# The key-side forget bias of one attention group: from a broadcast tensor added on VectorE to an extra matmul into the score bank

## The reference

```python
def dense_causal_attention(q, k, v, scale, fcum=None):
    ...
        s = jnp.einsum('bhqd,bhkd->bhqk', qi, k, preferred_element_type=jnp.float32) * scale
        if fcum is not None:
            s = s + args[2][..., :, None] - fcum[:, :, None, :]
        qpos = i * Q_BLOCK + jnp.arange(Q_BLOCK)
        s = jnp.where(kpos[None, :] <= qpos[:, None], s, NEG_INF)
        p = jax.nn.softmax(s, axis=-1)
        return jnp.einsum('bhqk,bhkd->bhqd', p.astype(v.dtype), v)

def fox_mixer(q, k, v, f_logit, b_f):
    log_f = jax.nn.log_sigmoid(f_logit.astype(jnp.float32) + b_f.astype(jnp.float32))
    fcum = jnp.cumsum(log_f, axis=1).transpose(0, 2, 1)
```

## Time and profile before

| | |
|---|---|
| median of three runs | 3331.21 us |
| the profiled execution, its own time | 3331.21 us |
| its span, first to last instruction | 3329.4 us |
| TensorE matmul busy | 3042.9 us, 91% |
| VectorE busy | 1924.9 us, 58% |
| ScalarE busy | 1279.9 us, 38% |
| GpSimd busy | 372.0 us, 11% |
| mean granted TensorE clock | 0.987 of full speed |
| fox heads, from the first score to the last | about 178 to 222 us |

### The profile page before, as it was taken

How to read it: one execution, slowest core, us unless ns; L and a number is a source line. 1 busy time by engine, 2 the same in 40 slices (tenths; PEclk the granted TensorE clock), 3 DMA queues, 4 the chain that set the end, 5 groups by cost and what they waited for, 6 DMA issues and landing times.

```text
span 3329.4 us, 43391 instructions
## 1 busy us (share of the span) xinstructions
PE 3042.9 (91%) x18036; PEld 2379.4 (71%) x18036; DVE 1924.9 (58%) x2872; ACT 1279.9 (38%) x2355; POOL 372.0 (11%) x364
## 2 busy tenths in 40 slices
PE   8999999999999999999999999999987777777776
PEld 8888978999999999989999997444442233333332
DVE  6565665555555555676765454555555555555654
ACT  4554554444434345565544352222222222222222
POOL 1001000000000001100000011222232222222221
PEclk9999999999999999999999999999999989999999
DMA  7454446555555555544445448999999999999997
GB/s 216 174 195 158 161 151 215 179 188 179 188 179 186 181 182 198 195 165 153 152 177 203 140 152 333 430 431 430 431 430 431 430 429 431 431 431 431 431 431 337
DMA packets 94785, 912.65 MB, mean 274 GB/s; under 512 B 10416, under 2 KB 14904, under 8 KB 19580
## 3 DMA queue, kind: packets, MB, share of 16 engines
q0 software_dynamic: 38128, 541.61, 38.1%
q1 hardware_dynamic: 48816, 344.95, 29.9%
q10 hardware_dynamic: 7644, 23.30, 2.2%
HBM read 900.38 MB, written 9.45 MB: 273 GB/s over the span
## 4 chain that ended last, share of the span: by engine, by line
PE 66%; DMA 23%; DVE 6%; ACT 4%; issue 1%; ACTq 0%; POOL 0%; DVEq 0%; POOLq 0%
PE sums L555 15%; PE sums L557 14%; PE sums L556 14%; DMA area<-in_uv,cst 13%; PE sums L1025 9%; DMA hT<-in_uv,cst 5%; DMA ringx<-in_uv,cst 3%; PE sums L981 2%; DVE area L2261 1%; PE sums L617 1%; DVE wl L1690 1%; PE sums L619 1%; PE sums L618 1%; ACT cst L1070 1%; ACT area L1070 1%
## 5 line engine op out<-in xcount | busy, mean ns | idle before, releaser
L1690 DVE TENSOR_TENSOR wl<-ring,wh 128x1024 fp32r<-128x1024 f32 x612 | 749.9, 1230 | 597.2 <-ACT wh L1070 596.3
L1070 ACT ACTIVATE wh<-ring 128x1024 fp32r<-128x1024 f32 x612 | 643.5, 1054 | 460.2 <-PE sums L557 404.5
L1070 ACT ACTIVATE cst<-cst 128x1 f32<-128x1 f32 (+2 forms) x786 | 234.2, 299 | 903.6 <-DVE cst L2261 845.1
L1025 PE MATMUL sums<-area,cst 128*128 128x512 f32 x984 | 457.4, 611 | 100.1 <-ACT cst L1070 99.8
L1025 PEld LDWEIGHTS sums<-area,cst 128*128 128x128 f32 x984 | 182.7, 193 | 356.6 <-issue 189.6
L2261 DVE CUSTOM_DVE_ANT_0 area<-area 128x2048 f32<-128x2048 f32 x123 | 281.8, 2291 | 254.5 <-DMA area<-in_uv,cst 254.5
L555 PE MATMUL sums<-normed,wh 128*128 128x256 f32 x1440 | 407.0, 283 | 0.2 <-DVE wl L1690 0.2
L557 PE MATMUL sums<-normed,wl 128*128 128x256 f32 x1440 | 406.7, 282 | 0.0
L1025 PE MATMUL sums<-ringx,cst 128*128 128x512 f32 x656 | 303.8, 609 | 60.0 <-ACT cst L1070 60.0
L555 PE MATMUL sums<-hidden,wh 128*128 128x256 f32 x1024 | 289.8, 283 | 0.0
L556 PE MATMUL sums<-hidden,wh 128*128 128x256 f32 x1024 | 289.8, 283 | 0.0
(11 more groups left out here) (335 smaller groups left out, 5753.6 us busy)
## 6 DMA issues: line engine op xcount, KB each, us to landing
ring<-in_w_in_a SPq DMA_DIRECT2D x66, 1024.0 KB, 4.9
ring<-in_w_up SPq DMA_DIRECT2D x64, 1024.0 KB, 4.9
ring<-in_w_down SPq DMA_DIRECT2D x64, 1024.0 KB, 4.9
ring<-in_w_out SPq DMA_DIRECT2D x32, 1024.0 KB, 5.0
ring<-in_w_in_b SPq DMA_DIRECT2D x16, 1024.0 KB, 4.9
ring<-in_w_xk SPq DMA_DIRECT2D x16, 1024.0 KB, 5.2
ring<-in_w_xv SPq DMA_DIRECT2D x16, 1024.0 KB, 5.1
ring<-in_w_xq SPq DMA_DIRECT2D x16, 1024.0 KB, 5.0
```

What stands on the lines that cost most here:

```text
L1025: mm = te.matmul(sums[t][:, 512 * i:512 * i + 512], diag[:, n % 2, :], v[:, 512 * i:512 * i + 512], start=False, stop=n % 128 == 127)
L1070: return sc.activation(out, in_, f, **kw)
L1690: ve.tensor_tensor(wl[:, j % 3, :], ring[:, load % 3, j % 2 * 1024:j % 2 * 1024 + 1024], wh[:, j % 3, :], ALU.subtract).then_inc(lo_in, 1)
```

## The change

The broadcast of the key-side term goes. Each score matmul of a fox head is left open for accumulation, and a second matmul adds to the same columns of the same bank: its weights are the head's block of `sel8` (8 partitions, 128 columns), its moving operand `nfcum` (8 partitions, 128 or 256 columns). The product is row h of `nfcum` on all 128 partitions. VectorE's L1813 then adds the query column and the causal mask, which is the constant that MLA heads use. The DMA to HBM and back, their waits, the buffer `fb` and the eight `mask_keys` are removed; the count on `bias_in` becomes 48 where it was 96; GpSimd's wait for `brow_out` moves behind its eight subtractions.

```diff
-        fb = flat(bias)[:, 2048:5120].rearrange("p (h n) -> p h n", h=8)
-        nfcum_d = nc.dram_tensor("fox_rows", (8, T), F32).ap()
...
-                                bias=fb[:, h, :], f=h, out=cqm[:, 4 + h // 2, :]))
+                                bias=causal, f=h, out=cqm[:, 4 + h // 2, :]))
...
                             hd, bank = heads[x + e], banks[3 + e]
+                            f = "f" in hd
                             mm = te.matmul(bank[:, a:b], hd["q"][:, qt * P:(qt + 1) * P], hd["k"][:, 0:b - a],
-                                           start=True, stop=True)
+                                           start=True, stop=not f)
+                            if f:
+                                mm = te.matmul(bank[:, a:b], C("sel8", 128, 128 * hd["f"], 8), nfcum[:, 0:b - a],
+                                               start=False, stop=True)
                             if qt == 1:
                                 mm.then_inc(scored, 1)
...
-                on.wait_ge(bias_in, 96)
+                on.wait_ge(bias_in, 48)
...
                         if "f" in hd:
                             on.wait_ge(fcol, 2)
-                            on.wait_ge(fox_v, hd["f"] + 2)
...
-                        if x + 1 < n and "f" in heads[x + 1]:
-                            mask_keys(x + 1)
...
-            def mask_keys(h):
-
-                ve.tensor_tensor(fb[:, h, :], fb[:, h, :], causal, ALU.add).then_inc(fox_v, 1)
...
-                on.wait_ge(bias_in, 48)
-                mask_keys(0)
                 yield from attention(fox_heads(), 8)
...
             sum_squares("attn")
-            on.wait_ge(brow_out, 16)
-            on.wait_ge(fox_in, 1)
-            gp.dma_start(nfcum_d, nfcum[:, :]).then_inc(bias_in, 16)
-            on.wait_ge(bias_in, 16)
-            for y, n in ((0, 128), (128, 256)):
-                gp.dma_start(fb[:, :, y:y + n], bass.AP(nfcum_d.tensor, 0, [[0, 128], [T, 8], [1, n]])
-                             ).then_inc(bias_in, 16)
             for k in range(1, 16, 2):
                 on.wait_ge(xh_in, SPLIT_H["mem"] + k + 1)
                 gp.tensor_tensor(m1l[:, k, :], memT[:, k, :], m1h[:, k, :], ALU.subtract).then_inc(xl_p, 1)
+            on.wait_ge(brow_out, 16)
             on.wait_ge(moved, 2)
```

## The result

The changed kernel takes 3355.86 us (median of 4 runs, 3352.16 to 3357.42) beside 3331.62 us for the kernel before (4 runs, 3328.55 to 3336.02): ratio 1.0066, 95% interval 1.0055 to 1.0079. That is 24 us slower. The forecast of 3344.5 us had the direction and little over half of the size, and the median lies above the range.

A forecast was written before the change was run, and what follows sets the result against it. TensorE, full in the fox heads, was taken to bound the kernel; removals cost nothing, four pairs add 3.3 us each, 13.3 in all: 3331.2 + 13.3 = 3344.5 us. Own range 3341 to 3348, wider range 3336 to 3350.

The forecast's parts named there:

- The bound: Fox heads, 178 to 222.5 us: TensorE sets the time, busy 44.50 of 44.50 us, never waiting for another engine.
- What is removed: Eight VectorE mask additions, 4.4 us, and the DMA round trip: covered by TensorE's work, so costed at nothing.
- The rival of VectorE's relief: Fox heads: VectorE was near the bound, so the eight masks count 4.4 us, giving 3326.8 us; chance 0.03.
- The 4.18 us of a pair: A pair of fox scores on TensorE: 4 x 0.415 + 4 x 0.63 = 4.18 us, where it was 0.86.
- 0.20 us for each change of shape: TensorE, between 8-row and 64-row matmuls: each border costs 0.09 us of emptying plus 0.11 of bare weight load.
- The cheap rival: Fox pairs: 8 rows beside 64 are no change of shape, TensorE keeps its pipeline full; 3336.4 or 3338.9 us, chance 0.15.
- The lock of VectorE and TensorE: Fox pairs: banks held longer and L1813's wait delay split weights, 1 to 2 us a pair; 3348 to 3353 us, chance 0.06.
- The step that failed: Low clock of 0.50 at 304 to 308 us: that stretch moves as a whole, its length differing by a microsecond or two.
- a predicted 13.3 us: TensorE, four pairs of fox scores: 3.3 us added to each pair, 13.3 us in all.

The follow-up runs named there:

- the one-pair kernel: The changed kernel with the selector matmuls of the first two fox heads alone, the other six heads' key bias left out; 3339.14 us, ratio 1.0017.

## Why the prediction was wrong in size

**The bound** was right. TensorE stayed busy for 63.70 of 63.70 us and no other engine ended a wait of it.

**What is removed** was rightly costed at nothing, by experiment: 1.0005 (0.9996 to 1.0014) without the selectors. The rival of VectorE's relief (3326.8 us) is out. VectorE's busy time in the fox stage fell by 3.5 us (39.00 to 35.46) where 4.4 were forecast; it bought nothing either way.

**The 4.18 us of a pair** were right to 0.02 in the second and third pair, and so was its smallest brick, 0.20 us for each change of shape. It came from two places of one timeline, and four kernels now bear it out: pairs with 9 changes at 4.16, with 5 at 2.75, with 5 and side-by-side selectors at 2.11, and with 5 and doubled selectors at 4.06. The split of the 0.20 into 0.09 of emptying and 0.11 of bare load was not tested by itself. The cheap rival is out too.

**The lock of VectorE and TensorE** did not come: the splits idled 17.0 us instead of 7.7, more slack and not less.

**The step that failed** is the one on the clock: the sum has no term for it in the fox stage, and its only word on a low clock is about the stretch from 304 to 308 us. It read: "That stretch moves as a whole; how long it lasts may differ by a microsecond or two." I had looked for the clock only where it was already low, and summed the new pairs and all that follows them at 2.4 GHz because the window of before stood at 1.00. The clock is the missing term of the sum: 13.4 us at half clock inside the fox stage, 6.0 us of time, beside a predicted 13.3 us. The kernel with 128-row selectors is the forecast made real: all the changes of shape but one, no fall of the clock, 12.6 us on the stage.

The Trainium skill, TensorE: Matmul & The Clock Gate, Part 1: The HAM clock gate, describes a clock that idleness of TensorE brings down. The trace of before fits that, 0.50 after a window busy for 2.00 of 4 us; the changed kernel's busy row does not, since TensorE is busy for 4.00 of 4.00 us from 178 to 182 and from 222 to 226 us, ahead of the first and the last fall. But that row counts each matmul until its results are written and so hides the holes. By the prices of the passes, 8 x 0.107 + 8 x 0.215, an estimate, only 2.57 of a pair's 4.16 us are streaming. The holes don't order the kernels either: the selectors of 128 rows stream in 2.57 of 3.87 us and had no fall, the doubled ones, by the same estimate, in 0.64 + 2.57 = 3.21 of 4.06 us, and the clock fell at all four pairs. A reader who looks for idle time alone would make my mistake.

**Behind the stage** the difference shrinks from 18.8 us (fifteenth split) to 16.4 (121st). A part of it is the low stretch near 300 us that both kernels have. Windows of the kernel before:

```profile
302.60:312.80 10.20, 10.20 (x142) 9.90 (x139) 0.00 (x0) 0.64 (x3) 0.00 (x0) 0.50 0.98 331
319.70:323.00 3.30, 3.30 (x27) 3.26 (x25) 1.23 (x1) 1.13 (x2) 0.00 (x0) 0.50 0.00 0
```

and of the changed kernel:

```profile
322.50:332.50 10.00, 10.00 (x111) 9.70 (x109) 0.75 (x1) 1.70 (x4) 0.00 (x0) 0.50 1.00 359
```

It lasted 13.5 us before and 10.0 after, worth some 1.7 us. That much of the microsecond or two was right. The rest of the 2.4 us, and the 1.8 us that are back by the end, are not followed here.

**What stays open.** The two medians of the result are 24 us apart, those of all executions on record 20.5, the two traced executions 18.2. The mean granted clock does not settle the rest: it is 0.984 to 0.988 in the 23 executions and 0.985 to 0.990 in those of the kernel before, and it also counts stretches in which TensorE does not set the time. What other traces do show is one place where executions differ, far from the fox heads. The kernel without selectors has the fox stage of before, but its traced execution (3337.19 us) is 6.0 us longer, and 4.1 of these are there by the hundredth split, at 557 us. Its clock is low twice on the way, where it stays at 1.00 in the traces of before and of the changed kernel:

```profile
480.50:487.40 6.90, 6.90 (x21) 5.71 (x21) 4.02 (x11) 3.86 (x7) 0.00 (x0) 0.51 0.50 167
545.40:548.80 3.40, 3.14 (x15) 3.17 (x16) 1.68 (x3) 0.90 (x3) 0.00 (x0) 0.50 1.04 410
```

So the traced execution of the changed kernel, the fastest of 23, may simply be one without them. Whether the others have these stretches, or more of them in the fox stage, is not seen, as each kernel has one trace. Which property of the few-row passes brings the clock down is open as well, and so is the part of the holes: no kernel has few-row passes without changes of shape. The runs separate 8 and 32 rows from 128 in the same order, and a few-row pair of 2.75 us from few-row pairs of 4.06 to 4.2, and no more.

## What to carry to other kernels

Before work is moved onto a TensorE that is already full, read two prices from the trace: what a pass costs with the shape of its neighbours, and what it costs with another (here 0.20 us more at each border, as much as streaming two passes of 128 columns). Then look at the granted clock behind it too, since here the clock took 6 us on top of 13. If a small operand must be multiplied in between, pad it to the tile shape of the matmuls around it and keep it on their partitions; that took this change from 3.3 us a pair to 0.75. And work that an idle engine does for nothing, like the eight masks and the broadcast here, is worth nothing when it is removed.

## What was not expected of the hardware

- TensorE's granted clock went to 0.50 while its row was busy without a gap, in or behind pairs of scores of 4.1 us made of passes on 8 or 32 rows and on 64. It did not with 128 rows in place of the 8 (3.87 us a pair), nor with 8-row passes in pairs of 2.75 us.
- How long the clock stayed down varied between kernels with the same first pair (3.4 and 6.8 us at half clock), and it could go down within the pair (3.5 us after the first load in the one-pair kernel) or behind it; one pair of the changed kernel was followed by no fall.
- 32 rows next to 64 empty TensorE just as 8 or 128 next to 64 do (4.16 us a pair both with 8 and with 32 rows).
- Two row groups of 64 work side by side also where the program alternates between them and between score and selector: the 16 passes of a pair took 1.61 us, where streaming them one after another would be 8 x 0.107 + 8 x 0.215 = 2.57 us.
